# Start of a fused two-block kernel: x loaded behind four weight units, its squares behind the fifth split, and the value product moved ahead of the gate product

## The reference

```python
h = rmsnorm(x, norm_mix_pre[l])
proj = h @ w_in[l]
gq, gk, gv, gg1, gr, pu, mq, mk, mv, gates = jnp.split(proj, splits, axis=-1)
ya = gla_mixer(gq, gk, gv, gg1, gr, gla_w_g2[l], gla_b_g[l], gla_norm[l]) @ w_branch_a[l]
```

## Time and profile before

| | |
|---|---|
| median of 3 runs | 1143.47 us |
| profiled execution | 1144.22 us |
| its span | 1142.4 us |
| TensorE busy | 1118.3 us, 98% |
| VectorE busy | 712.7 us, 62% |
| ScalarE busy | 557.2 us, 49% |
| GpSimd busy | 22.8 us, 2% |
| HBM traffic over the span | 185 GB/s |
| mean granted clock of TensorE | 0.995 of full speed |

### The profile page before, as it was taken

One profiled execution on the slowest core, in us unless ns is written; L12 is line 12 of the kernel. 1 busy time (PEld: TensorE's weight loads), 2 busy tenths in 40 slices (PEclk: granted clock), 3 DMA queues, 4 the chain that ended last, 5 costly groups with the idle time before them and its releaser, 6 DMA issues.

```text
span 1142.4 us, 18412 instructions
## 1 busy us (share of the span) xinstructions
PE 1118.3 (98%) x7650; PEld 1010.4 (88%) x7650; DVE 712.7 (62%) x1077; ACT 557.2 (49%) x836; POOL 22.8 (2%) x43
## 2 busy tenths in 40 slices
PE   8999999999999999999999999999999999999996
PEld 7888778789999988899998899888788989999985
DVE  5686765867666646556665555565556656666652
ACT  5543574546444445545354455444734545444542
POOL 0000400000000000000000000000000000000000
PEclk9999999999999999999999999999999999999999
DMA  7645444655665655576866567323375335655661
GB/s 281 196 158 171 173 167 155 220 193 169 193 205 190 228 195 166 179 277 199 287 213 216 187 212 240 101 93 107 107 253 171 130 111 186 202 189 189 202 211 58
DMA packets 63374, 210.79 MB, mean 185 GB/s; under 512 B 7387, under 2 KB 14731, under 8 KB 62396
## 3 DMA queue, kind: packets, MB, share of 16 engines
q1 hardware_dynamic: 63004, 209.53, 55.2%
q10 hardware_dynamic: 288, 0.10, 0.0%
HBM read 206.44 MB, written 5.26 MB: 185 GB/s over the span
## 4 chain that ended last, share of the span: by engine, by line
PE 85%; DVE 6%; ACT 4%; DMA 3%; issue 1%; POOL 0%; SPq 0%; DVEq 0%; POOLq 0%; ACTq 0%
PE ps L835 13%; PE ps L838 13%; PE ps L837 13%; PE ps L827 13%; PE ps L829 12%; PE ps L828 12%; PE ps L989 2%; DMA raw<-in_wflat 2%; PE ps L856 1%; DVE wlo L1596 1%; DVE wlo_b L1596 1%; PE ps L978 1%; DMA x<-in_x 1%; PE ps L903 1%; ACT junk L1300 1%
## 5 line engine op out<-in xcount | busy, mean ns | idle before, releaser
L835 PE MATMUL ps<-hT_hi,whi_b 128*128 128x256 f32 x1392 | 387.6, 278 | 4.7 <-DVE wlo_b L1596 4.7
L837 PE MATMUL ps<-hT_hi,wlo_b 128*128 128x256 f32 x1392 | 384.6, 276 | 0.0
L838 PE MATMUL ps<-hT_lo,whi_b 128*128 128x256 f32 x1392 | 384.6, 276 | 0.0
L1596 DVE TENSOR_TENSOR wlo_b<-raw,whi_b 128x1024 fp32r<-128x1024 f32 (+1 forms) x184 | 219.7, 1213 | 116.9 <-ACT whi_b L1275 116.6
L1596 DVE TENSOR_TENSOR wlo<-raw,whi 128x1024 fp32r<-128x1024 f32 x176 | 212.3, 1224 | 114.3 <-ACT whi L1275 113.5
L835 PEld LDWEIGHTS ps<-hT_hi,whi_b 128*128 128x128 f32 x1392 | 261.4, 188 | 8.7 <-issue 5.6
L837 PEld LDWEIGHTS ps<-hT_hi,wlo_b 128*128 128x128 f32 x1392 | 261.4, 188 | 0.3
L838 PEld LDWEIGHTS ps<-hT_lo,whi_b 128*128 128x128 f32 x1392 | 261.3, 188 | 0.0
L1275 ACT ACTIVATE whi<-raw 128x1024 fp32r<-128x1024 f32 x176 | 181.7, 1056 | 111.5 <-PE ps L829 90.1
L1275 ACT ACTIVATE whi_b<-raw 128x1024 fp32r<-128x1024 f32 (+1 forms) x184 | 184.6, 1042 | 38.0 <-PE ps L829 15.3
L827 PE MATMUL ps<-whi,hT_hi 128*128 128x512 f32 (+1 forms) x272 | 109.1, 401 | 3.1 <-DVE m_gqk L1660 1.6
(11 more groups left out here) (316 smaller groups left out, 1263.3 us busy)
## 6 DMA issues: line engine op xcount, KB each, us to landing
raw<-in_wflat SPq DMA_DIRECT2D x358, 512.0 KB, 4.1
wide<-scratch SPq DMA_DIRECT2D x1, 2048.0 KB, 9.9
m_w<-in_cmp_k_w SPq DMA_DIRECT2D x4, 512.0 KB, 6.9
m_w<-in_cmp_v_w SPq DMA_DIRECT2D x4, 512.0 KB, 6.9
m_alibi<-in_c_alibi SPq DMA_DIRECT2D x1, 1536.0 KB, 7.3
m_xT<-in_xT SPq DMA_DIRECT2D x4, 256.0 KB, 5.9
x<-in_x SPq DMA_DIRECT2D x2, 512.0 KB, 8.3
m_memT<-in_memT SPq DMA_DIRECT2D x1, 1024.0 KB, 5.9
```

Of the source, the lines that this page charges most:

```text
L835: e.matmul(o, hi[:, k, c], xs.h(k0 + k), start=first and k == 0 and f % 2 == 0, stop=False, skip_group_check=True)
L837: e.matmul(o, lo[:, k, c], xs.h(k0 + k), start=False, stop=False, skip_group_check=True)
L838: r = e.matmul(o, hi[:, k, c], xs.l(k0 + k), start=False, stop=last and k == kt - 1, skip_group_check=True)
L1596: e.tensor_tensor(slot(wlo, u)[:, 0:k * n], r, h.bitcast(F32), ALU.subtract).then_inc(*w_lo.did(u))
```

## The change

Three edits, all before or at the first products. In `weight_chunks`, gv comes before g1, so that gv has units 4 to 7 and g1 unit 8; gr keeps units 9 to 12. In `order`, the last feature quarter stands alone ahead of unit 0, the first squares stand behind split 3, the second squares with the spawning of `rest0` behind split 4 (the fifth), and the products go qk, gv, end of gv, end of qk, g1, end of g1. In SyncE's program xT3 and unit 3 are loaded ahead of x0 and x1.

The list then begins, from quarter 2 and split 2 on: quarter 3, unit 0; split 3, first squares, unit 1; split 4, second squares, `rest0` spawned, unit 2; step 1 (root); split 5, unit 3, step 2; split 6, unit 4 (gv), step 3; split 7, unit 5, step 4 ("across"); split 8, unit 6; split 9, unit 7; end of gv, end of qk; split 10, unit 8 (g1), end of g1; late constants, "gla" spawned, gr. Banks: qk 0 and 1, gv 2 and 3, g1 0, gr 1 and 2.

```diff
     add("qk", "w_in", _cols((256, 512), (0, 256)), D)
-    for name, a, b in (("g1", 1024, 1040), ("gv", 512, 1024), ("gr", 1040, 1552),
+    for name, a, b in (("gv", 512, 1024), ("g1", 1024, 1040), ("gr", 1040, 1552),
                        ("pu", 1552, 2064), ("mq", 2064, 2576), ("mk", 2576, 3088), ("mv", 3088, 3600)):
...
-    def more_x():
-        yield from do("squares0_0")
-        yield from do("quarter0_3")
-
     yield from do("begin")
     for n in range(3):
         yield from do(f"quarter0_{n}")
         yield from split_to(n)
-    yield from product("qk", {0: more_x, 1: x_squared}, open_end=True)
+    yield from product("qk", {0: lambda: do("quarter0_3"), 1: lambda: do("squares0_0"), 2: x_squared}, open_end=True)
+    yield from product("gv")
+    yield "end", "qk", 0, 0
     yield from product("g1")
-    yield "end", "qk", 0, 0
-    yield from product("gv")
     yield from do("late_constants")
     spawn("gla")
...
-            for i in range(3):
+            for i in range(4):
                 load(f"xT{i}", xT[:, 2 * i:2 * i + 2, :], io["xT"][:, 2 * i:2 * i + 2, :])
                 fetch(i)
             for t in range(2):
                 load(f"x{t}", x[:, t, :], xin[:, t, :])
-            load("xT3", xT[:, 6:8, :], io["xT"][:, 6:8, :])
-            fetch(3)
```

## The result

The changed kernel took 1141.34 us (median of 20 runs, 1138.76 to 1143.38), the kernel before in the same sessions 1143.7 us (20 runs, 1140.21 to 1145.36). The ratio is 0.9981 with a 95% interval of 0.9972 to 0.9989: by the ratio 2.2 us faster, between 1.3 and 3.2. I had forecast 1.2 us faster. The measured time lies in the stated range, the direction is right, and the gain is larger than the sum.

A forecast was written before the change was run, and what follows sets the result against it. TensorE, busy 98% of the span, bounds the kernel, so only its gaps can be won. Won 2.57 us less lost 1.37 nets -1.2: from 1143.47 to 1142.3 us, range 1140.3 to 1144.2.

The forecast's parts named there:

- The clock: TensorE's clock was taken to be at full speed throughout; the sum had no term for it.
- Gap A: TensorE's idle time between qk's third and fourth units, 16.90 to 17.84; forecast to go, 0.94 us won.
- Gap B: TensorE's idle time between "across" and the value product, 23.97 to 25.60, over a bank; forecast to go, 1.63 us won.
- Gap C: New TensorE gap ahead of gv's first unit, from unit 4 landing at 17.8; 0.67 us lost.
- the sign that I had set myself: The forecast counts as wrong if unit 4's first matmul comes at 19.7.
- the other sign: The forecast counts as wrong if unit 4's first matmul comes after 21.5.
- Gap D: New TensorE gap ahead of gv's second unit, due at 23.2, forecast to start at 23.68; 0.5 us lost.
- "Across" costs its 0.6 us: "Across", now behind gv's second unit, costs 0.6 us as before, and 0.1 at most for the wait.
- The sum: Won 2.57 us, lost 1.37 us, net -1.2 us; gr's first unit at about 35.4 in place of 36.66.
- Downstream: TensorE's later gaps at 60.80 and 68.80 should move along unchanged; taken as 0, bounds -1.8 to +1.8 us.

The follow-up runs named there:

- after_wide_later: The changed kernel with SyncE's wait for the copy to `wide` three steps later (6 in place of 3); ratio 0.999 against the kernel before.
- root_later: The changed kernel with the root of x behind split 5 instead of split 4; ratio 0.9975 against the kernel before.
- all_three: The changed kernel with root behind split 5, msk and cst late, and the wait for `wide` later; ratio 0.9986 against the kernel before.
- after: The changed kernel itself, first measurement and profile; 1141.34 us, ratio 0.9981 against the kernel before.
- after_again: The changed kernel profiled once more, the same program; no time or ratio given, logits at 38.81 us.
- products_only: The kernel before with only the products and their weights swapped (qk, gv, end of qk, g1), loads and squares as before; ratio 0.9982.
- loads_only: The kernel before with only the order of the loads changed, xT3 and unit 3 ahead of x; ratio 1.0033.
- x_behind_unit3: The kernel before with the changed kernel's loads, last feature quarter ahead, both squares behind split 3, products still qk, g1, gv; ratio 1.0006.
- constants_late: The changed kernel with msk and cst (0.49 MB) loaded among the late constants instead of ahead of unit 4; ratio 0.9977 against the kernel before.
- both: The changed kernel with root behind split 5 and msk and cst late, together; ratio 0.998 against the kernel before.
- unit4_late: The changed kernel with the row of norm_mix_post (0.52 MB) loaded ahead of unit 4 instead of among the late constants; ratio 1.0005 against the kernel before.
- before_wide_later: The kernel before with SyncE's wait for the copy to `wide` three steps later (6 in place of 3); ratio 0.9995.

## Why the prediction was right, and where it was not

*The clock.* I took it to be full throughout. It wasn't: the first profile of before has two stretches at 1.2 GHz, in the stretches table above, and its mean of 0.995 is not full speed. The sum has no term for the clock, and that is part of what it misses.

*Gap A goes.* Right: 16.98 forecast as 16.9. ScalarE took the last feature pair at 11.20 and split 3 at 12.16, each 0.4 us before my time.

*Gap B goes.* Right in mechanism: with the products alone the wait is gone, and the logits come 1.14 us earlier while A stays, with gv's first unit waiting for its lower half instead. The size was a little small: from the start of "across" to gv's next matmul it was 2.23 us before (23.37 to 25.60) and is 0.36 now (25.96 to 26.32), so 1.87 us are won, not 1.63.

*Gap C, 0.67 us.* The place was right, the term mis-sized through its landing. I bounded unit 4's landing by 16.64 and 18.24 and took 17.8; it was 17.3, 18.6 and, in after_wide_later, 18.6, so the upper bound was broken twice. The gap was 0, 1.3 and 1.2 us. From the landing on, everything held where TensorE had to wait: 2.4 us to the first matmul. By the sign that I had set myself (I am wrong if unit 4's first matmul comes at 19.7) the first profile, with 19.71, speaks against the term; the other two, at 21.02 and 20.96, don't reach the other sign, 21.5.

*Gap D, 0.5 us.* Right in three profiles (0.48, 0.47, 0.46), and root_later shows its cause.

*"Across" costs its 0.6 us.* Too much: matmuls before and behind it are 0.6 us apart (25.72 to 26.32) where the pace is 0.23, so it costs 0.37.

*The sum, -1.2 us.* At the logits the three profiles with the changed start are 2.03, 0.66 and 0.77 us ahead of the first profile of before: mean 1.15. That this meets 1.2 so closely is in part luck: gap B won 0.2 more than I had, gap C cost some 0.2 more, and a single execution lies 0.4 to 0.8 off. And the parts did not share it as I had it. I put 0.94 down to gap A and 1.63 to gap B. The runs show that x behind unit 3 and its squares win nothing clear of the noise alone (1.0006), and nothing on top of the products (logits 38.32 and 38.33): A is exchanged for C and D, since the root now hangs on later bytes.

*Downstream, 0.* The gaps near 60 and 68 us moved along, as said. That nothing else takes or gives was wrong as a statement on one execution: between 60 and 540 us four of the profiles lose 0.2 to 0.6 us, between 540 and 600 us they lose 0 to 1.8 us (against after_wide_later and all_three, which have no gap there; before lost 0.95), and between 690 and 850 us none, one or two stretches at 1.2 GHz cost 1.6 us each.

*The measured 2.2 us against 1.2.* The interval, 1.3 to 3.2, only just leaves out the sum. The changed kernel's profiles (after, after_again, after_wide_later) had no stretch at 1.2 GHz between 690 and 850 us; all the others had two, products_only one. But the changed kernel doesn't avoid them as a rule. Each run lists its mean granted clock: the profiles without such a stretch have 0.997 or 0.998, those with two 0.992 to 0.995, and 9 of the changed kernel's 20 runs have 0.994 or 0.995.

These clocks also part what the start won from what the clock gave. Over the 88 runs of the kernel before in the sessions of the experiments, a clock lower by 0.001 goes with 1.0 us more. Taking that off the difference of the mean times, against the kernel before in the same session, leaves an estimate in us, with its 95% interval from redrawing the runs:

```
                     at equal clock            at the logits
after                -1.2 (-1.6 to -0.7)       -1.15, mean of three
loads_only            2.0 (1.5 to 2.5)          1.88
x_behind_unit3        0.2 (-0.3 to 0.7)        -0.21
products_only        -0.9 (-1.4 to -0.5)       -1.14
root_later           -1.8 (-2.6 to -0.9)       -2.46
constants_late       -2.3 (-2.8 to -1.8)       -2.74
both                 -2.2 (-2.7 to -1.7)       -2.71
unit4_late           -0.2 (-0.8 to 0.5)         1.47
before_wide_later    -0.5 (-1.0 to 0.2)        -0.32
after_wide_later     -0.6 (-1.3 to 0.0)        -0.77
all_three            -2.7 (-3.3 to -2.2)       -2.90
```

(For after the 88 runs stand in, because only one of the 20 runs beside it has its clock on record. In unit4_late what its runs lost to the clock at the start is taken off too, 1.6 us in its profile.) So by this estimate the start's gain is the forecast 1.2 us. Of the measured 2.2, some 0.6 is the clock's: its mean is 0.9960 over the changed kernel's runs and 0.9954 over the 88. That is twice the standard error of the difference, 0.0003, so whether the change itself brings it stays open. The rest, 0.4 us, is as much as the kernel before differs between its sessions (means of 1143.4 and 1143.0).

It also answers what the ratios blur: with the constants out of unit 4's way the kernel is about 1 us faster again than the changed one, since the gaps C and D are gone. In all_three the ratio doesn't show it because its ten runs had a lower clock, 0.9945.

## What to carry to other kernels

When a wait is taken out by bringing other work forward, ask what the bytes and the small chain behind it now stand in front of: here the reordering of the loads exchanged one gap for two. A product that needs no result of a normalization is best put where a bank would otherwise be waited for; the products alone gave nearly all of the gain. And ask what stands in the queue ahead of the first transfer that matters: moving 0.49 MB of constants behind it was worth about as much as the whole change. Differences of one or two us in a kernel of a thousand are read from the same matmul in several profiles and from runs at equal clock, not from one span.

## What the runs showed of the hardware

The same 512 KB transfer, issued at the same time (8.6 us) behind the same bytes, landed 8.7 us after its issue in one execution and 10.0 in two others, while the core's DMA moved 404 and 402 GB/s between 14 and 19 us in the first two. The constants ahead of it were issued up to 0.5 us later in the slow cases, but in root_later, with nearly as late an issue (7.09 us against 7.21 and 7.33), the transfer landed after 8.8. So the rate doesn't fix a landing to better than 1.3 us.

TensorE at 2.4 GHz fell to 1.2 GHz after an idle time of 2.44 us in unit4_late. Idle times of 1.63 us (kernel before) and 1.2 us (after, once more) at nearly the same place did not do that, and neither did one of 2.56 us in loads_only, one unit earlier. The length of the idle time alone doesn't decide it in these traces. In the attention stage the clock fell, for 1.6 us of loss each time, from one of 701 to 714, 762 to 772 and 813 to 818 us in some executions and not in others, also between two executions of the same program.
